# One encoder kernel: its loop over two layers unrolled, the norm by token tile, and an order of steps for each engine

## The reference

```
for l in range(2):
    h = rms(x) * norm_g[l]
    p = h @ w_in[l]                       # 1024 x 11808, cut into the inputs below
    y_a = gated delta rule, both directions: convolution of 5 taps, silu, 4 heads, chunks of 64
    y_b = neighbourhood attention with a bias table, 8 heads
    y_c = attention with axial rotary, 4 heads on 2 key heads
    y_d = mLSTM, both directions, 4 heads, chunks of 64
    each y times silu(its z); y_d also times sigmoid(o)
    merged = sum over n of sigmoid(gate_n) * (y_n @ w_branch[l][n])
    x = x + merged @ w_out[l]
```

## Time and profile before

| | |
|---|---|
| median of 3 runs | 983.67 us (981.82 to 983.68) |
| profiled execution: span | 982.1 us |
| median less that span (start and end around it) | 1.6 us |
| PE busy, 7206 matmuls | 903.4 us, 92% |
| DVE busy | 672.2 us, 68% |
| ACT busy | 497.9 us, 51% |
| POOL busy | 203.0 us, 21% |
| instructions | 19657 |
| HBM, over the span | 146 GB/s |

### The profile page before, as it was taken

How to read it: one execution, slowest core, us unless ns; L and a number is a source line. 1 busy time by engine, 2 the same in 40 slices (tenths; PEclk the granted TensorE clock), 3 DMA queues, 4 the chain that set the end, 5 groups by cost and what they waited for, 6 DMA issues and landing times. The chain is left out here.

```text
span 982.1 us, 19657 instructions
## 1 busy us (share of the span) xinstructions
PE 903.4 (92%) x7206; PEld 750.8 (76%) x7206; DVE 672.2 (68%) x1209; ACT 497.9 (51%) x990; POOL 203.0 (21%) x216
## 2 busy tenths in 40 slices
PE   3998999999899999999859899999998989999996
PEld 3986778787787788778658787788877768887775
DVE  3888795667368587587459887765762776866763
ACT  3545644553454565555246555544543645564651
POOL 0301221435220014121021111222542200322210
PEclk9989999999999999999959999999999999999999
DMA  7643634424376145467156346434333832544762
GB/s 205 204 135 118 203 119 131 129 90 127 90 174 190 48 150 168 130 179 228 65 133 187 124 138 209 127 111 141 105 108 98 208 124 86 152 149 129 234 195 65
DMA packets 101403, 140.13 MB, mean 143 GB/s; under 512 B 31022, under 2 KB 45494, under 8 KB 101174
## 3 DMA queue, kind: packets, MB, share of 16 engines
q1 hardware_dynamic: 94118, 137.80, 47.4%
q10 hardware_dynamic: 7184, 1.02, 0.6%
HBM read 135.63 MB, written 7.27 MB: 146 GB/s over the span
## 5 line engine op out<-in xcount | busy, mean ns | idle before, releaser
L1411 DVE TENSOR_TENSOR w_low<-ring,w_high 128x512 fp32r<-128x512 f32 x464 | 325.6, 743 | 112.5 <-ACT w_high L1098 112.4
L1098 ACT ACTIVATE w_high<-ring 128x512 fp32r<-128x512 f32 x464 | 274.0, 627 | 87.2 <-PE pj L605 44.3
L603 PE MATMUL pj<-w_high,h_high 128*128 128x512 f32 x592 | 245.1, 414 | 8.7 <-DVE w_low L1411 7.9
L605 PE MATMUL pj<-w_high,h_low 128*128 128x512 f32 x592 | 234.2, 396 | 0.0
L604 PE MATMUL pj<-w_low,h_high 128*128 128x512 f32 x592 | 234.1, 395 | 0.0
L603 PEld LDWEIGHTS pj<-w_high,h_high 128*128 128x128 f32 x592 | 113.4, 191 | 36.4 <-DVE w_low L1411 8.3
L605 PEld LDWEIGHTS pj<-w_high,h_low 128*128 128x128 f32 x592 | 112.9, 191 | 24.8
L604 PEld LDWEIGHTS pj<-w_low,h_high 128*128 128x128 f32 x592 | 113.4, 192 | 22.5 <-issue 1.0
L1103 ACT ACTIVATE big<-pair 128x512 f32<-128x512 f32 (+2 forms) x136 | 60.9, 482 | 77.0 <-PE pair L780 37.1
L603 PE MATMUL mb<-w_high,h_high 128*128 128x512 f32 x112 | 44.4, 397 | 3.1 <-DVE h_low L1860 3.1
L1933 POOL TENSOR_TENSOR big<-big,tab 128x256 f32<-128x256 f32 x40 | 34.6, 881 | 48.6 <-ACT big L1255 25.0
(11 more groups left out here) (282 smaller groups left out, 1553.6 us busy)
## 6 DMA issues: line engine op xcount, KB each, us to landing
ring<-in_w_in SPq DMA_DIRECT2D x368, 256.0 KB, 3.2
ring<-in_w_branch SPq DMA_DIRECT2D x64, 256.0 KB, 3.0
ring<-in_w_out SPq DMA_DIRECT2D x32, 256.0 KB, 3.2
big<-skew SPq DMA_DIRECT2D x32, 128.0 KB, 3.7
skew<-lines SPq DMA_DIRECT2D x16, 224.0 KB
out_x<-btm SPq DMA_DIRECT2D x12, 256.0 KB, 3.8
btm<-out_x SPq DMA_DIRECT2D x8, 256.0 KB, 4.7
tab<-in_table SPq DMA_DIRECT2D x1, 1408.0 KB, 7.8
```

The source lines that it names most:

```text
L603: mm(o, r32(a), r32(b), start=start, stop=False, skip_group_check=True)
L605: return mm(o, r32(a_low), r32(b), start=False, stop=stop, skip_group_check=True)
L1098: f(r32(w_high[:, u % PARTS]), ring[:, u % RAW], ACT.Copy).then_inc(w_rounded, 1)
L1411: tt(r32(w_low[:, u % PARTS]), ring[:, u % RAW], w_high[:, u % PARTS], ALU.subtract).then_inc(w_split, 1)
```

## The change

The two layers are written out one after the other in one program with one block. Semaphores are not cleared; each wait adds what the layers before have counted (`at`). SCHEDULE gives way to ORDER: for each engine a list for the start, one for the layer, one for between the layers and one for the end. Splits (`split+3`), evictions (`take:za:0@1`), adds of a branch (`add:`) and products of a single tile (`za:0:0+4@0`) are words of their own there.

The norm goes by token tile and by half rows: `square` on ACT for each half, `scale` on POOL and DVE for each tile, with norm_g as a row over all partitions, so that only the taps are still transposed (`taps`). The squares and the scale of tile 0 for layer 1 stand between the layers. Products begin with za, tile 0 first. The last block of out does tile 0's units 2 to 7 ahead of tile 1's. The first two units of a layer go to two more slots in y_high and y_low (`part_slots`). SP issues layer 1's parameter loads during layer 0; for layer 0 ACT issues its 15 loads first of all. Stores of the result are issued by quarter as they are done. x is saved later, with conv:2's units; bias loads come later too.

```diff
-SCHEDULE = """
-    norm conv:0:0+4 conv.0 conv:1:0+4 conv.1 silu.0 gatecols conv:2:0+4 gatecols_turn conv.2 silu.1 conv:3:0+4 conv.3 silu.2 a_turn.0 rope za:0:0+2
-    za:0:2+2 silu.3 conv:4:0+4 cols conv.4 a_turn.1 a_norm silu.4 conv:5:0+4 za:0:4+2 a_scale conv.5 za:0:6+2 silu.5 a_qkt c:0:0+2 a_kkqk a_turn.2
...
+ORDER = {
+    "PE": ("""
+
+    """, """
+        turn_h.0.0 turn_h.0.1 turn_h.1.0 taps turn_h.1.1 za:0:0+4@0 za:0:4+2@0 za:0:6+2@0 za:0:0+2@1 za:0:2+4@1 za:0:6+2@1 conv:0:0+4 conv:1:0+4
+        conv:2:0+4 conv:3:0+4 gatecols c:0:0+2 gatecols_turn c:0:2+2 conv:4:0+4 cols a_turn.0 a_turn.1 conv:5:0+4 scan_v.0 c:0:4+2 c:0:6+2 c:1:0+2
+        c:1:2+2 a_qkt c:1:4+2 a_kkqk a_turn.2 c:1:6+2 rows.0 rows.1 zc:0:0+2 zc:0:2+2 zc:0:4+2 zc:0:6+2 solve0.0 solve0.1 b:0:0+2 b:0:2+2 b:0:4+2
+        t1.0.1 t1.1.1 c_qkt update.0.1 update.1.1 c_score.0.0 rows.2 b:0:6+2 t1.0.2 t1.1.2 c_turn.0.0 c_score.0.1 update.0.2 b:1:0+2 update.1.2
+        b:1:2+2 c_mix.0.0 t1.0.3 t1.1.3 c_turn.0.1 update.0.3 b:1:4+2 c_score.1.0 t1.0.4 b:1:6+2 update.1.3 c_mix.0.1 update.0.4 c_turn.1.0 b:2:0+2
+        b:2:2+2 b:2:4+2 t1.1.4 b:2:6+2 t1.0.5 rows.3 c_score.1.1 update.1.4 zb:0:0+2 t1.1.5 zb:0:2+2 update.0.5 update.1.5 c_mix.1.0 zb:0:4+2 uw.0
+        c_turn.1.1 zb:0:6+2 qd.0 uw.1 d:0:0+2 c_mix.1.1 c_out.0 solve0.2 c_out.1 qd.1 d:0:2+2 solve0.3 t1.2.1 scan_o.0 update.2.1 d:0:4+2 t1.3.1
...
+        b_turn_in a_out.0 a_out.1 gate:0,1:4+2 d_rows.0 gate:0,1:6+2 d_rows.1 branch:0,0:0+2 branch:0,0:2+2 d_rows.2 d_rows.3 gate:2,0:0+2 d_prep
+        b_score.0.0 gate:2,0:2+2 b_score.0.1 b_turn.0.0 gate:2,0:4+2 gate:2,0:6+2 b_mix.0.0 b_score.1.0 b_turn.0.1 branch:0,1:0+2 branch:0,1:2+2
+        b_mix.0.1 b_score.1.1 b_turn.1.0 gate:2,1:0+2 gate:2,1:2+2 gate:2,1:4+2 gate:2,1:6+2 branch:2,0:0+2 branch:2,0:2+2 b_mix.1.0 b_turn.1.1
...
+        branch:3,0:0+2 branch:3,0:2+2 branch:3,1:0+2 merge_turn.0 branch:3,1:2+2 out:0:0+2 merge_turn.1 out:0:2+2 out:0:4+2 out:0:6+2
+    """, """
+        out:1:0+2 out:1:2+6@0 out:1:2+1@1 out:1:3+1@1 out:1:4+2@1 out:1:6+2@1
+    """, """
+        out:1:0+2 out:1:2+6@0 out:1:2+6@1
+    """),
+    "ACT": ("""
+        split+1 square.0.0 square.0.1 square.1.0 split+3
+    """, """
+        split+1 square.1.1 turn_h.0.0 turn_h.0.1 turn_h.1.0 turn_h.1.1 split+1 taps split+4 take:za:0@0 take:za:0@1 split+1 small split+7
+        take:conv:0@0 split+6 take:conv:1@0 split+2 silu.0 split+2 take:conv:2@0 take:conv:3@0 gatecols silu.1 split+5 gates_exp split+3 silu.2
...
+        next_square.0.0 split+8 next_square.1.0 next_square.0.1
...
+    "DVE": ("""
+        split+3 scale.0 split+1
+    """, """
+        scale.1 turn_h.0.0 turn_h.0.1 turn_h.1.0 turn_h.1.1 split+5 take:za:0@0 split+4 take:za:0@1 split+6 small split+5 taps conv.0 split+3 silu.0
+        split+1 conv.1 conv.2 split+1 gates_in split+4 gates_out conv.3 silu.1 silu.2 silu.3 split+2 conv.4 split+5 a_norm.0 a_norm.1 split+6 a_scale
+        conv.5 silu.4 silu.5 split+2 gain_a split+4 rows_arg.0 rows_arg.1 split+1 rows.0 rows.1 split+3 c_prep split+3 take:zc:0@0 split+1
+        take:zc:0@1 split+2 c_rotate.0 c_rotate.1 split+2 update.0.1 update.1.1 split+1 rows_arg.2 c_score.0.0 split+5 c_score.0.1 split+2 cols
+        update.0.2 update.1.2 update.0.3 c_mix.0.0 c_score.1.0 split+4 c_mix.0.1 window split+2 update.1.3 split+4 update.0.4 rows_arg.3 c_score.1.1
...
+        split+6 take:out:1@0 split+2 take:out:1@1 next_scale.0
...
+def part_slots(plan):
+
+    slots, turn, last = [], 0, {}
+    first = -1
+    for n, unit in enumerate(plan):
+        if unit[0] != first:
+            first, at = unit[0], n
+            for k in range(EXTRA if n else 0):
+                last[PARTS + k] = max(i for i in range(n) if plan[i][1] == "branch")
+        slot = PARTS + n - at if n - at < EXTRA else turn % PARTS
+        turn += n - at >= EXTRA
+        slots.append((slot, last.get(slot)))
+        last[slot] = n
+    return slots
 
 
...
+        def at(signal, n):
+
+            return signal, now[0] * signals[signal.num] + n
...
-        with nc.Fori(0, DEPTH) as layer:
-            with nc.Block() as block:
+            for layer in range(DEPTH):
+                now[0] = layer
+                before.update(filling)
+                filling.clear()
...
+                load_x(sp, 0)
+                for unit in range(2):
+                    load_unit(sp, unit)
+                load_x(sp, 1)
+                for unit in range(2, RAW):
+                    load_unit(sp, unit)
+                load_rows(act, 0)
+                load_cols(act, 0)
...
+                    def turn_h(t, q):
+                        pe.wait_ge(*at(h_ready, 2 * t + q + 1))
+                        b = mb[2 * t + q]
+                        pe.wait_ge(*room(b, ("hT", t, q)))
+                        turn4(b, [xh[:, t, (4 * q + k) * P:(4 * q + k + 1) * P] for k in range(4)])
...
+                        if unit == unit_of("conv", 2, 0):
+                            sp.wait_ge(*at(h_ready, 4))
+                            if layer:
+                                sp.wait_ge(*at(x_back, 0))
...
+                        params = unit - unit_of("branch", (BRANCHES[3], 0), 0)
+                        if layer < DEPTH - 1 and 0 <= params < 12:
+                            if params == 0:
+                                load_rows(sp, layer + 1)
+                            elif params == 1:
+                                load_cols(sp, layer + 1)
+                            else:
+                                load_param(sp, layer + 1, params - 2)
+                    if layer == DEPTH - 1:
+                        for block_, t in ((0, 0), (0, 1), (1, 0), (1, 1)):
+                            sp.wait_ge(*released(("pj", "out", block_, t)))
+                            for half in range(2):
+                                c = CHUNKS[t][half]
+                                sl = slice(block_ * WB, (block_ + 1) * WB)
+                                sp.dma_start(out[0, c * C:c * C + C, sl], x[rows_of(half), t, sl]).then_inc(stored, 16)
+                        sp.wait_ge(stored, 16 * 8)
...
+                    def square(t, q, of=layer):
+
+                        if of == 0:
+                            act.wait_ge(x_loaded[t], 32)
+                        else:
+                            act.wait_ge(*(released if of > layer else released_before)(("pj", "out", q, t)))
+                        sl = slice(q * WB, (q + 1) * WB)
+                        f(xh[:, t, sl], x[:, t, sl], ACT.Square, accum_out=ssx[:, t, q:q + 1]).then_inc(x_squared, 1)
+
+                    def turn_h(t, q):
+                        act.wait_ge(*filled(("hT", t, q)))
+                        v = (slice(None), slice(4 * q, 4 * q + 4), slice(t * P, (t + 1) * P))
...
+                    if layer == 0:
+                        for n in range(PARAMS):
+                            load_param(act, 0, n)
...
+                    def scale(t, of=layer):
+
+                        dve.wait_ge(rms_x, NT * of + t + 1)
+                        if t == 0:
+                            dve.wait_ge(g_row_in, 16 * (of + 1))
+                        for q in range(2):
+                            sl = slice(q * WB, (q + 1) * WB)
+                            stt(xh[:, t, sl], x[:, t, sl], rsx[:, t:t + 1], g_row[:, sl], ALU.mult, ALU.mult).then_inc(h_ready, 1)
+
+                    def turn_h(t, q):
+                        b = bank_of(("hT", t, q))
+                        dve.wait_ge(*at(h_rounded, 2 * t + q + 1))
+                        v = (slice(None), slice(4 * q, 4 * q + 4), slice(t * P, (t + 1) * P))
+                        stt(r32(h_low[v]), four(b.t), float(D) ** 0.5, h_high[v], ALU.mult, ALU.subtract).then_inc(b.free, 1)
...
+                    def scale(t, of=layer):
+
+                        pool.wait_ge(x_squared, 4 * of + ((2 if of == 0 else 3) if t == 0 else 4))
+                        rs = rsx[:, t:t + 1]
+                        link(pool.tensor_scalar(rs, ssx[:, t, 0:1], ssx[:, t, 1:2], D * EPS, ALU.add, ALU.add))
+                        pool.tensor_tensor(rs, rs, neg_half[:, 0:1], ALU.pow).then_inc(rms_x, 1)
...
-            nc.all_engine_barrier()
-            nc.sync.sem_clear(range(min(nums), max(nums) + 1))
-            nc.all_engine_barrier()
...
```

More of the change, by code:

```diff
@@ L54 @@
 WB, CUN = 512, 4
-RAW, PARTS, LEAD = 6, 6, 4
+RAW, PARTS, EXTRA = 6, 6, 2
 TILE_OF = (0, 1, 1, 0)
@@ L179, in weight_plan @@
-    return plan
+    for layer, stages in enumerate(layers):
+        for name, *args in stages:
+            if name != "proj" or args[4] == (1,):
+                continue
+            kind, arg, u, n = args[:4]
+            if kind == "branch":
+                col = arg[1] * WB
+            elif kind == "gate":
+                col = GATES + arg[0] * D + arg[1] * WB
+            else:
+                col = first[kind] + arg * (CW if kind == "conv" else WB)
+            plan += [(layer, kind, arg, u + i, col) for i in range(n)]
```

(5 more changed lines are left out.)

961 lines of the change are left out of this document (466 added, 495 removed).

## The result

The changed kernel takes 966.05 us (median of 4 runs, 963.95 to 968.08), against 982.75 for the kernel before in the same comparison: a ratio of 0.983, 95% interval 0.9805 to 0.9855. The forecast was 938.4, from 918 to 966, so the result lies just past the slow end of the range: 17 us are won where some 45 were expected. The profiled execution has a span of 966.0 us, against 982.1 before.

What follows compares the result with a forecast made beforehand. PE, busy 92% of the span, was taken to bound the kernel by its own order of work. 982.1 - 12.7 - 3.0 + 0.4 - 30 = 936.8 us profiled, 938.4 for the median, range 918 to 966.

Steps and rivals of the forecast that it cites:

- The start: Before the first product: ACT's fifteen issues end at 9.6, first product at 20.7 against 20.28; +0.4 us, bounds -3 and +2.
- The boundary: Between the layers: loop's end and parameter loads go, token tile 1's chain of 5.2 us stays of 17.9; saves 12.7 us.
- The end: Behind the last add: stores by quarter, 5.4 us against 8.1; taken as 3.0 us less, bounds 2 and 4.
- The convolution stage: Waits and low-clock stretches of 23.7 us in both layers fall to about 8; saves 15.7 us.
- Inside a layer, the rest: Other waits and low clock inside the layers: 14 of 25.8 us go, a bit over half.
- The other half of my count: Low-clock stretches inside the layers cost half their length if PE had work throughout: 13.6 us.
- The two signs that I had named for a wrong forecast: Waits inside the layers still adding to 35 us, or a boundary over 8 us.
- the inside stays: Rival: DVE's load decides inside the layers in either order, only 15.3 us go, 968; chance 0.18.

Runs made afterwards that it cites:

- cols_sp: Changed kernel, but SyncE issues the two narrow-column loads behind its table load and ACT keeps thirteen issues; 956.98 us.
- params_sp: Changed kernel, but SyncE issues layer 0's ten parameter loads behind its table load, leaving ACT five issues; 957.97 us.
- old_order: Changed kernel with the old SCHEDULE's common order inside each layer, written out as four lists; 976.66 us.
- conv_stage_only: Changed kernel with its new lists up to zc's first product and the old common order from there to the layer's end; 982.96 us.
- c_prep_first: Changed kernel with one word moved on POOL: c_prep ahead of t1.0.1 instead of behind it; 959.87 us.
- splits_moved: Changed kernel with only splits moved on DVE and ACT, ahead of the stalls that wait for them; 965.06 us.
- qkt_later: On top of c_prep_first, PE takes c_qkt behind the updates and two units of b, DVE two splits between its rotations; 962.46 us.
- act_params: Changed kernel, but ACT issues layer 1's fourteen parameter loads at the start of layer 1, not SyncE during layer 0; 973.54 us.
- cols_last: Changed kernel, but ACT issues the two narrow-column loads behind the ten parameters instead of ahead of them; 964.29 us.
- sp_waits: Changed kernel, but SyncE waits until all ten parameters have landed before loading units 2 to 5 and the table; 967.27 us.

## Why the prediction was right or wrong

The result is 29.2 us above the forecast of the span (966.0 to 936.8). The start has 11.0 of them and the inside of the layers behind zc 16.7; the convolution stage and the boundary have 1.8 and 0.7, and the end gives 1.0 back.

**The start: wrong, a term mis-sized.** I took ACT's fifteen issues as fifteen times the 0.59 us of the earlier trace rows and ended them at 9.6; they end at 20.4. The first product is 11.4 us later than before where I had +0.4, with -3 to +2 as bounds. The mean hid what a row of the kernel before showed, right behind the same two column loads, three times its neighbours:

```profile
10.28 0.47 ACTq L1373 DMA_DIRECT2D mid<-in_w_in  x1
10.90 1.44 ACTq L1377 DMA_DIRECT2D small<-in_dn_norm_g  x1
12.43 0.40 ACTq L1377 DMA_DIRECT2D small<-in_ml_norm_g  x1
```

Moved to the very start, behind norm_g and the taps on the same queue, that load meets x, six units and the table, and costs 9.3. With the columns or the parameters elsewhere the first product comes at 21.7 and 21.0 (cols_sp, params_sp), near the 20.7 that I worked out, but that is luck: ACT's issues end at 7.9 and 3.6 there, not at 9.6, and what fills the time is the wait for tile 1 of x, which my sum did not have. The Trainium skill's "DMA: Bandwidth & Descriptors", section "Issuing engines are not separate DMA queues", which I had weighed, calls the time to initiate a DMA "usually small relative to the DMA itself"; this trace is a case in which it is not, 9.31 us for a load of 64 KB that lands 16.0 us after its issue began. What I had drawn from its first half, that tile 1's x lands later, holds: in params_sp ACT waits for it until 12.76.

**The boundary: right.** 12.0 won, 12.7 forecast, by the chain that was named. Its parts, by experiment: 7.1 the loads, 1.2 the norm by tile, 3.7 the rest, with the 2.7 of the long issue to be moved from the first to the last. **The end: right in kind**, 4.0 for 3.0: from the last add it takes 4.0 us, less than the 5.4 that I allowed.

**The convolution stage: right in the mechanism, in part by luck in the size.** 13.9 won, 15.7 forecast from the lists alone; old_order has 4.4 of the 13.9 with the old list, so the new ones won 9.5. PE idles 2.7 us there in each layer, where I had 2.4, and falls to the low level once for 3.4 us, as forecast (layer 1 starts with 4.4 more, which belong to the boundary).

**Inside a layer, the rest: wrong.** I took 14 of 25.8 us, "a bit over half" (PE's rows of waits add to 70.4 as printed, not to my 70.7, which changes nothing). From zc to the last product the layers take 751.1 us, against 748.7 before: a loss of 2.4 (from none to 4.8 over the nine traces with these lists). The steps that failed are that more than half of these waits and low stretches would go, and that a wait which goes is time won. Three things stood in its place. First, the convolution stage was covered with c's products, which had been the cover of the delta rule's start; I counted what each stage wins and not what it takes from the next. This is read from the lists and from where conv_stage_only waits, not shown by a run of its own. Second, POOL's list puts c_prep behind t1.0.1, a step that waits for ACT; that alone is 6.2 us (c_prep_first). Third, where one wait is closed the next opens: splits_moved took 4.2 us of waits away and won 1, qkt_later none. I had named this effect, and sized it by a guess. With the POOL word moved the same sum is 746.1, so even then the rest wins 2.6 and not 14. Over both layers, convolution stage included, PE's idle time did fall, from 40.6 us to 28.3, and that is about all that the inside won (11.5 by the table). The other half of my count was busy time at the low level. Those stretches, up to the last product, add to 23.9 us instead of 47.8, and PE is busy in them for 21.5 us instead of 33.8. By half of the difference its busy time should have fallen some 6 us, yet it is 903.6 after and 903.4 before. old_order narrows this down: it is busy for 897.2, of which 17.0 at the low level. After is 6.4 us above that, 2.2 of it by the clock, so some 4 us lie in the new lists and not in the program. What in the lists does it stays open. The two signs that I had named for a wrong forecast did not show: the waits inside add to 28 us, not 35, and the boundary is under 8. Neither looked at the start or at PE's busy time.

The rival "the inside stays" had 968, the nearest of my numbers, and was wrong in its reason: the inside won 11.5 us, and the start lost as much.

## What to carry to other kernels

Ahead of the first work of an engine, cost DMA issues one by one and not by their mean, and look at the issue that stands behind a load of many small pieces; give such loads to a queue that nobody waits for. When products are moved to cover one stage, write down what they covered before. In a list of its own for each engine, look for a step that waits with a short step behind it whose result another engine needs: moving one such word was worth 6.2 us here, where all the lists together had won 10.6.

## What the hardware showed that I had not expected

An issue can block its engine for 9.31 us. Four runs place it: it stands right behind the two column loads (after, act_params) or on the second of them (cols_last, cols_sp). The columns alone do not make it: with the DMA engines at 0.16 ahead of it the issue behind them took 0.47 us (layer 1 of before). The DMA engines' busy share during the long ones, as the view of stretches gives it, was 1.07 (9.31 us, after), 1.00 (5.12, sp_waits) and 0.82 (3.12, act_params). One rival is untested: wherever the issue was over 3 us, norm_g over all partitions (512 KB) and the taps had gone to the same queue or, in cols_sp, x, six units and the table, and no run takes those away.

POOL's operations are long beside DVE. The same 128x256 operation of t1 takes 0.74 us and, while DVE rotates, 3.10 (1.03 in the short case above); c_prep's first operation takes 0.33 and 0.80 after, 0.21 before and 3.47 in conv_stage_only. The Trainium skill, "SBUF — State Buffer", section "Who interferes with whom", says that a DVE instruction with two SBUF inputs contends with a GpSimd instruction that reads SBUF, and that the order of issue decides who blocks. DVE's rotation, which multiplies two tiles in SBUF, is of that kind, and the rows agree in kind: POOL's operations are long while DVE's rotation runs beside them. No run here varies it alone. I had costed POOL's steps by their shortest rows.
